# Stick-breaking attention on Trainium2: the sums over later key blocks as two fp32r products instead of one fp32 product

## The reference

```python
z = einsum('bhtd,bhsd->bhts', q_blk, k_blk) * scale
strict = s_pos < t_pos
log_beta = log_sigmoid(z)
log_1m_beta = where(strict, log_sigmoid(-z), 0.0)
between = cumsum(log_1m_beta, axis=3, reverse=True) - log_1m_beta
weights = where(strict, exp(log_beta + between), 0.0)
out = einsum('bhts,bhsv->bhtv', weights, v_blk)
```

## Time and profile before

| | |
|---|---|
| time, median of 3 runs | 2455.09 us (2452.5 to 2456.87) |
| the profiled execution's own time | 2456.69 us |
| its span | 2454.9 us |
| mean granted clock of TensorE | 0.983 |
| PE busy over the span | 96% |
| the stage of the change | about 2210 to 2353 us from the span's start |

### The profile page before, as it was taken

How to read it: one execution, slowest core, us unless ns; L and a number is a source line. 1 busy time by engine, 2 the same in 40 slices (tenths; PEclk the granted TensorE clock), 3 DMA queues, 4 the chain that set the end, 5 groups by cost and what they waited for, 6 DMA issues and landing times.

```text
span 2454.9 us, 45626 instructions
## 1 busy us (share of the span) xinstructions
PE 2363.5 (96%) x17622; PEld 1881.5 (77%) x17622; DVE 1389.8 (57%) x1747; ACT 939.0 (38%) x1418; POOL 1294.0 (53%) x768
## 2 busy tenths in 40 slices
PE   7999979999999999999999999999999999998798
PEld 5777769996877788888888877887877777773367
DVE  4377685556257666666665434564454366655464
ACT  3133352222335444444444212232252135557641
POOL 3332100001666677777777789789676445530045
PEclk9999999999999999999999999999999999999999
DMA  4311000000432333333332655465321111122033
GB/s 146 80 37 34 27 16 4 5 4 19 146 113 94 120 111 111 108 115 116 110 107 92 234 199 189 168 209 186 130 92 62 45 48 48 53 73 86 1 118 122
DMA packets 106616, 231.79 MB, mean 94 GB/s; under 512 B 7368, under 2 KB 46664, under 8 KB 106312
## 3 DMA queue, kind: packets, MB, share of 16 engines
q1 hardware_dynamic: 82496, 169.89, 20.8%
q10 hardware_dynamic: 23944, 59.46, 7.5%
HBM read 190.52 MB, written 38.80 MB: 93 GB/s over the span
## 4 chain that ended last, share of the span: by engine, by line
PE 73%; DVE 9%; ACT 6%; POOL 5%; issue 3%; DMA 3%; ACTq 0%; DVEq 0%; POOLq 0%; SPq 0%
PE ps L834 11%; PE ps L1310 6%; PE ps L1311 6%; PE ps L1312 6%; PE ps L1467 6%; PE ps L930 5%; PE ps L1439 4%; PE ps L1490 3%; PE ps L1348 2%; PE ps L1350 2%; PE ps L1351 2%; DMA w_raw<-wall 2%; POOL w_lo L621 2%; ACT ab L152 2%; POOL w_hi L618 2%
## 5 line engine op out<-in xcount | busy, mean ns | idle before, releaser
L618 POOL TENSOR_TENSOR w_hi<-w_raw,small 128x1024 fp32r<-128x1024 f32 x156 | 305.9, 1961 | 738.4 <-PE ps L834 274.6
L621 POOL TENSOR_TENSOR w_lo<-w_raw,w_hi 128x1024 fp32r<-128x1024 f32 x156 | 431.2, 2764 | 12.3
L683 POOL TENSOR_TENSOR slot_lo<-scr,slot_hi 128x512 fp32r<-128x512 f32 x116 | 160.6, 1395 | 85.5 <-ACT slot_hi L152 85.5
L834 PE MATMUL ps<-x_hi,w_hi 128*128 128x512 f32 x448 | 176.0, 402 | 5.3 <-POOL w_lo L621 2.3
L834 PE MATMUL ps<-x_lo,w_hi 128*128 128x512 f32 x448 | 172.1, 393 | 0.0
L834 PE MATMUL ps<-x_hi,w_lo 128*128 128x512 f32 x448 | 172.0, 393 | 0.0
L152 ACT ACTIVATE slot_hi<-scr 128x512 fp32r<-128x512 f32 x116 | 73.4, 633 | 195.6 <-POOL scr L693 77.7
L1310 PE MATMUL ps<-t_hi,slot_hi 128*128 128x512 f32 x348 | 135.5, 389 | 0.4 <-ACT p L152 0.4
L1311 PE MATMUL ps<-t_lo,slot_hi 128*128 128x512 f32 x348 | 135.4, 389 | 0.0
L1312 PE MATMUL ps<-t_hi,slot_lo 128*128 128x512 f32 x348 | 135.4, 389 | 0.0
L639 POOL COPY xx<-rmask 128x512 f32<-128x512 f32 x16 | 11.8, 749 | 227.5 <-PE ps L1133 174.6
(11 more groups left out here) (389 smaller groups left out, 6471.9 us busy)
## 6 DMA issues: line engine op xcount, KB each, us to landing
w_raw<-wall SPq DMA_DIRECT2D x191, 512.0 KB, 3.5
f_raw<-f_spill SPq DMA_DIRECT2D x62, 512.0 KB, 4.5
f_spill<-cg SPq DMA_DIRECT2D x30, 512.0 KB, 3.4
v_raw<-wall SPq DMA_DIRECT2D x29, 512.0 KB, 3.5
ada_w<-wada ACTq DMA_DIRECT2D x24, 512.0 KB, 3.9
fill_spill<-stage ACTq DMA_DIRECT2D x24, 256.0 KB, 2.0
x_in<-xT ACTq DMA_DIRECT2D x8, 512.0 KB, 8.8
x<-xT ACTq DMA_DIRECT2D x8, 512.0 KB, 4.2
```

Of the source, the lines that this page charges most:

```text
L618: nc.gpsimd.tensor_tensor(w_hi[:, u, :, :], w_raw[:, u, :, :], sm["one"].unsqueeze(2).to_broadcast([P, KT, P]), ALU.mult).then_inc(S("w_hi ...
L621: nc.gpsimd.tensor_tensor(w_lo[:, u, :, :], w_raw[:, u, :, :], w_hi[:, u, :, :].bitcast(F32), ALU.subtract).then_inc(S("w_split"), 1)
L683: tt_p(slot_lo[i][:, :, :], src, slot_hi[i][:, :, :].bitcast(F32), ALU.subtract).then_inc(later("s_lo")[0], 1)
L834: last = mm(ps[:, 2 * u + h, :], w[:, u, k, :], x[:, k, h * 512:(h + 1) * 512], start=(k == 0 and w is w_hi and x is hi), stop=(k == KT - ...
```

## The change

The running sum is split by VectorE into a high part `acc_hi`, which is the sum rounded to fp32r, and a low part `acc_lo`, which is the rest, also as fp32r. Both are then multiplied by the all-ones matrix, held as fp32r in `ones_r`, in two fp32r products that add onto the same PSUM columns. The split is a copy and a subtraction per element with b > 0 and has a place of its own in VectorE's order, after `later_keys(n)` and, where z is ahead, after `soft(n + 2)`. PE's wait on `sb_acc` now stands for the split of element n - 2. For b = 0 `later_keys` does nothing, where before it still added and copied in p = 0 (n = 14 and 15). `later_keys` no longer waits for `sb_sp`. The scratch tile `sq_h2` moves to make room, and a wait for the last `remainder` is put after `gated(6)`.

```diff
-        sq_h = [at("sq_h", [P, 4, T], 6)[:, k, :] for k in range(4)] + [at("sq_h2", [P, 2, T], 16)[:, k, :] for k in range(2)]
+        sq_h = [at("sq_h", [P, 4, T], 6)[:, k, :] for k in range(4)] + [at("sq_h2", [P, 2, T], 14)[:, k, :] for k in range(2)]
+        acc_hi = at("acc_hi", [P, 2, T], 16, F32R)
+        acc_lo = [at("acc_lo0", [P, T - P], 45, F32R), at("acc_lo1", [P, T - P], 49, F32R, off=spare + 512)]
+        ones_r = at("ones_r", [P, P], 45, F32R, off=3584)
...
+        def sums_made(n):
+
+            return n + 1 - 2 * (n // (2 * NB))
...
                 if b < NB - 1:
-                    pe.wait_ge(S("sb_acc"), n - 1)
+                    pe.wait_ge(S("sb_acc"), sums_made(n - 2))
                     for x, c, t in halves_of(b + 1):
-                        last = mm(z_out(n, x)[:, c:], sbmask[:, 1, :], lacc[:, e, t], start=False, stop=True,
+                        mm(z_out(n, x)[:, c:], ones_r[:, :], acc_hi[:, e, t], start=False, stop=True, skip_group_check=True)
+                        last = mm(z_out(n, x)[:, c:], ones_r[:, :], acc_lo[e][:, t.start - P:t.stop - P], start=False, stop=True,
                                   skip_group_check=True)
...
                 b, e = SB_STEPS[n // 2][1], n % 2
+                if b == 0:
+                    return
                 dve.wait_ge(S("sb_r"), n + 1)
-                dve.wait_ge(S("sb_sp"), n + 1)
-                if n // 2 == len(SB_STEPS) - 1:
-                    return
                 if b < NB - 1:
                     tt(lacc[:, e, (b + 1) * P:], lacc[:, e, (b + 1) * P:], spl[:, e, (b + 1) * P:], ALU.add)
-                vcopy(lacc[:, e, b * P:(b + 1) * P], spl[:, e, b * P:(b + 1) * P]).then_inc(S("sb_acc"), 1)
+                vcopy(lacc[:, e, b * P:(b + 1) * P], spl[:, e, b * P:(b + 1) * P])
+
+            def sums_split(n):
+
+                b, e = SB_STEPS[n // 2][1], n % 2
+                if b == 0:
+                    return
+                vcopy(acc_hi[:, e, b * P:], lacc[:, e, b * P:])
+                tt(acc_lo[e][:, (b - 1) * P:], lacc[:, e, b * P:], acc_hi[:, e, b * P:].bitcast(F32), ALU.subtract)\
+                    .then_inc(S("sb_acc"), 1)
...
             head_square(1)
+            dve.wait_ge(*landed("sbmask_in"))
+            vcopy(ones_r[:, :], sbmask[:, 1, :])
             for m in range(len(SB_STEPS)):
                 for n in (2 * m, 2 * m + 1):
                     later_keys(n)
                     if z_ahead(m + 1):
                         soft(n + 2)
+                    sums_split(n)
...
             gated(6)
+            dve.wait_ge(S("sb_r"), 2 * len(SB_STEPS))
             half_low(0, 2)
```

## The result

| | before | changed |
|---|---|---|
| median | 2453.97 us (22 runs) | 2458.93 us (22 runs) |
| ratio of the runs | 1 | 1.0020, 95% interval 1.0013 to 1.0028 |
| span of the profiled execution | 2454.9 us | 2458.5 us |

The changed kernel is about 5 us slower. The forecast was 1 us faster. The time lies within the stated range, but it moved 5 us the other way, so the cause was looked for.

A forecast was written before the change was run, and what follows sets the result against it. The stage was taken as bound by a loop of waits between engines, none full. Terms 0.35 - 0.2 + 1.0 - 1.25 - 0.4 - 0.5 sum to -1.0 us, giving a 2454.1 us median, range 2450 to 2460 us.

The forecast's parts named there:

- parts 1 and 2: Operation prices: TensorE saves 7.3 us of busy time over four heads; VectorE's stage load goes from 74.9 to about 104 us.
- (a): Stage start: the ones_r copy and first splits delay soft(3) and remainder(3), +0.35 us, between 0 and 0.9.
- (b): Step pairs with b = 4 and 3: TensorE's narrower sums bring back 0.2 us.
- (c): After n = 8: splits ahead of three head squares make soft(10) 2.4 us later, costing +1.0 us.
- (D): Rival: emptier TensorE waits longer and its clock falls, about 1.3 us each; three more falls give 2458 us; chance 0.1.
- (d): Next step pairs: two b = 1 splits, 3.7 us, fit VectorE's 4.36 us of idle time before soft; no cost.
- (f): Low-clock piece at 2306.05 us: -0.4 us; second pair has no head squares in one piece, so no repeated soft(10) delay.
- (e): At b = 0 of the first pair, both sums (n = 14 and 15) are on the path: -1.25 us.
- (g): Stage end: the last two sums save 1.24 us on TensorE, taken as -0.5 us, between -0.3 and -1.24.
- (C): Rival: VectorE becomes the bound through full-rate copies, or narrow fp32r products are no faster; about 2458 us, chance 0.2.
- (B): Rival: all six pieces on the path pay and VectorE's splits fit everywhere; -3.1 us, 2451.4 us, chance 0.2.

The follow-up runs named there:

- e5: The changed kernel plus 12 unread fp32r products in each of TensorE's two long waits, before remainder(10) and remainder(26); 2456.95 us, ratio 1.0012 to the kernel before.
- e3: The changed kernel with VectorE's split kept, but TensorE multiplying the unsplit fp32 sum by fp32 ones as before; 2456.56 us, ratio 1.0011 to the kernel before.
- e6: The changed kernel with head squares 3 to 5 after n = 15 to 17 and each split behind soft(n + 2); 2452.96 us, ratio 1.0003 to the kernel before.
- e4: The changed kernel without the split: running sum written as fp32r, both fp32r products taking it, so counted twice; 2454.05 us, ratio 0.9998 to the kernel before.
- e1: The changed kernel with head squares 3 to 5 moved from after n = 8 to after n = 15 to 17; 2452.12 us, ratio 0.9991 to the kernel before.
- e8: The changed kernel with head squares 3 to 5 late and unread products in three long TensorE waits; 2452.58 us, ratio 0.9999 to the kernel before.
- e10: The changed kernel with late head squares, splits behind soft(n + 2) and two groups of unread products; 2452.72 us, ratio 0.9993 to the kernel before.
- e7: The changed kernel with both operations of the split on GpSimd and the head squares where they were; 2455.55 us, ratio 1.0000 to the kernel before.

## Why the prediction was wrong

- **The prices (parts 1 and 2)** were right: 28 splits, 628 and 1092 ns at 896 columns, 103.4 us of VectorE in the stage. A narrow fp32r product was set too dear: 384 columns take 0.17 us and not 0.21, and with the narrower sums the products gain about 10.5 us at the full clock and not 7.3.
- **(a) and (b)**, +0.35 and -0.2: together +0.1 measured.
- **(c) is the step that failed.** It said "+1.0 us". It measured +4.0, and 4.5 in the other trace. It named the place, the order and the lateness of `soft(10)`, and the lateness alone is worth up to 1.4 us (e5), near the forecast. What it put at nothing is that the clock falls in the wait which it makes for TensorE, 5.14 us in one trace and 4.66 in the other, and everything behind is done at 1.2 GHz: 2.6 to 3.2 us more. The sum has no term for a new fall; that stood in rival (D) alone.
- **(d)**, "No cost": right in the first head pair as far as VectorE goes. The +0.4 there comes with a fall after m = 6, and e3 and e5, which have none there, take the 11.5 us of before.
- **(f)**'s second half, that (c) "is not repeated", failed too, +2.1: after n = 24 the splits, a `head_out` and a `gated` stand in front of `soft(26)`. The prediction looked only at the squares. e6 moved this back by the order alone. By e5's numbers nearly all of it is the fall behind that wait.
- **(e)**, -1.25: -1.0. **(f)**, -0.4: -0.6, from m = 12 to 13; the fall there is in all four traces of the two kernels. **(g)**, -0.5: -0.4. The last projection should have started 1 us earlier; the 1.1 us lost behind the last `weigh` were in no term.
- **The rivals.** (D) was right in its mechanism and too low in its chance, 0.1. It said that the change makes TensorE's waits longer, and it does, in two ways: by cheaper sums in front of the same wait (1.72 to 2.11 us in e4), and by VectorE's lateness (5.14 us). The falls came after waits of TensorE, as the Trainium skill, "TensorE: Matmul & The Clock Gate", section "What's actually happening", would have it. The rival priced a fall at 1.3 us and thought of them as strewn; the fall at (c) is in both traces of the changed kernel, and goes when the lateness goes (e1) or the wait is filled (e5). (C)'s mechanism, a copy at the single rate, didn't happen, but its sign did: VectorE binds where several of its operations stand in one piece. The terms of (C) and (D) had been kept apart as alternatives, where one caused the other. (B), -3.1 us, did not happen. In e4, without any split, the stage is no shorter, but the timed runs reach down to -3.9 us, so e4 speaks against (B) without excluding it; the 1.3 us estimated above are what speaks against it most.
- The rows of the table from the two traces without early falls add up to 4.8 us before rounding (152.52 - 147.75), and 1.1 us come behind the last `weigh`: 5.9 us, where the timed runs have 5.0 with an interval of 3.2 to 6.9.

What stays open: how many falls a given order gets. Their number varies between executions of the same code (2 and 4), so the falls in e4, e8 and e10 can't be put down to single causes with one trace each. The falls in this stage follow waits of TensorE of 1.0 to 5.1 us, but not every wait gets one: the wait of 2.4 us ahead of `head_mean(3)` is followed by a fall in most traces and by none in e3, e5 and e7. Which wait gets one is open; that the wait for `soft(10)` did, and what it cost, is shown by the products that removed it.

## What to carry to other kernels

When work moves from TensorE to VectorE, don't compare the totals: list what stands in one piece in front of each operation that TensorE waits for, and put the new work behind it. A wait of TensorE of some us must be priced twice, as the wait and as the slower work that may follow it, and cheaper products on TensorE make its waits longer by themselves. And a saving on an engine that sits in a loop of waits should first be tried alone, with the work that pays for it left out (e4): if that brings nothing, the rest need not be built.

## What had not been expected of the hardware

- Products that nobody reads made the stage shorter: 12 of them, 2.98 us in all, kept the clock at 1.00 and halved the product behind, 2.93 to 1.45 us. At another wait the same twelve were too many and cost 1.4 us of delay.
- While GpSimd worked on SBUF, VectorE's addition of two SBUF tiles of 512 columns took up to 1.50 us in place of 0.69.
- The same code reached the start of this stage at 2193.8 to 2206.7 us from the span's start in the traces of these kernels, which are alike up to there: a scatter of 13 us, larger than the effect under study.
